# Four value buffers in linear attention's output units, and an MLP's first differences alternating with the statistics

## What is computed

```python
def rms_norm(x, g):
    y = xf * lax.rsqrt(jnp.mean(xf * xf, axis=-1, keepdims=True) + RMS_EPS)
    return (y * g.astype(jnp.float32)).astype(x.dtype)

def even_mixer(u, ...):
    ...
    o = gla_chunked(q, k, v, log_alpha)          # 4 heads of 128 value channels
    o = rms_norm(o, gla_norm_g) * jax.nn.silu(g)
    mix = jnp.concatenate([rg_out, o.reshape(bn, sn, GLA_VDIM)], axis=-1)
    return mix @ w_out

for layer in range(2):
    ...                                          # mixer or attention -> y
    x = layer_norm(ALPHA * x + gate * y, ln_g[layer, 0], ln_b[layer, 0])
    u = x * (1.0 + scale) + shift
    y = jnp.square(jax.nn.relu(u @ mlp_w1[layer] + mlp_b1[layer])) @ mlp_w2[layer] + mlp_b2[layer]
    x = layer_norm(ALPHA * x + gate * y, ln_g[layer, 1], ln_b[layer, 1])
```

## Time and profile before

| | us |
|---|---|
| median of 3 runs | 4219.9 (4216.1 to 4227.6) |
| the profiled execution, its time | 4226.8 |
| the profiled execution, its span | 4225.0 |
| TensorE busy | 3917.6 (93%) |
| VectorE busy | 2061.9 (49%) |
| GpSimd busy | 1914.0 (45%) |
| ScalarE busy | 1175.5 (28%) |
| TensorE's granted clock, mean | 0.964 of full |
| value units, first and second pass | about 347 to 384 and 485 to 522 in the span |
| openings of the MLPs | about 543 to 593 and 2315 to 2367 in the span |

### The profile page before, as it was taken

One profiled execution on the slowest core, in us unless ns is written; L12 is line 12 of the kernel. 1 busy time (PEld: TensorE's weight loads), 2 busy tenths in 40 slices (PEclk: granted clock), 3 DMA queues, 4 the chain that ended last, 5 costly groups with the idle time before them and its releaser, 6 DMA issues.

```text
span 4225.0 us, 50589 instructions
## 1 busy us (share of the span) xinstructions
PE 3917.6 (93%) x18933; PEld 3176.9 (75%) x18933; DVE 2061.9 (49%) x3073; ACT 1175.5 (28%) x1889; POOL 1914.0 (45%) x748
## 2 busy tenths in 40 slices
PE   6898889999999999999987899999999889999997
PEld 4676777788877777777775777777877667888886
DVE  6754463434444654455555521211379666444445
ACT  5322231111114444444442311111223332222222
POOL 2433267566553412222211776446555376445352
PEclk9998999999999999999998999999999899999999
DMA  6321012322310101111100111111101111111110
GB/s 209 102 70 30 26 40 85 99 84 89 99 51 22 45 26 36 31 36 36 36 21 16 41 60 49 45 40 49 51 25 55 45 50 50 40 50 50 40 59 40
DMA packets 246725, 224.65 MB, mean 53 GB/s; under 512 B 12924, under 2 KB 194850, under 8 KB 246579
## 3 DMA queue, kind: packets, MB, share of 16 engines
q1 hardware_dynamic: 222496, 171.09, 13.4%
q10 hardware_dynamic: 24083, 51.54, 3.7%
HBM read 218.34 MB, written 4.26 MB: 53 GB/s over the span
## 4 chain that ended last, share of the span: by engine, by line
PE 80%; DVE 12%; ACT 3%; issue 2%; DMA 1%; ACTq 1%; DVEq 0%
PE PS L658 11%; PE PS L660 11%; PE PS L659 11%; PE PS L784 5%; PE PS L786 5%; PE PS L785 5%; PE PS L685 3%; PE PS L687 3%; PE PS L686 3%; PE PS L1138 3%; DVE ADMS L2115 2%; PE PS L1123 1%; PE PS L1108 1%; PE PS L1070 1%; PE PS L1050 1%
## 5 line engine op out<-in xcount | busy, mean ns | idle before, releaser
L3035 POOL TENSOR_SCALAR WH<-RAW 128x1024 fp32r<-128x1024 f32 x255 | 729.9, 2862 | 1317.8 <-PE PS L687 525.3
L658 PE MATMUL PS<-UH,WH 128*128 128x512 f32 (+1 forms) x2192 | 878.7, 401 | 16.2 <-DVE UL L2156 6.3
L659 PE MATMUL PS<-UL,WH 128*128 128x512 f32 (+1 forms) x2192 | 871.4, 398 | 0.0
L660 PE MATMUL PS<-UH,WL 128*128 128x512 f32 (+1 forms) x2192 | 871.3, 398 | 0.0
L3037 POOL TENSOR_TENSOR WL<-RAW,WH 128x1024 fp32r<-128x1024 f32 x255 | 621.1, 2436 | 21.3
L658 PEld LDWEIGHTS PS<-UH,WH 128*128 128x128 f32 (+1 forms) x2192 | 414.0, 189 | 122.8 <-issue 7.7
L2126 DVE TENSOR_TENSOR X<-PS,X 128x512 f32<-128x512 f32 x432 | 292.7, 687 | 435.2 <-PE PS L786 424.0
L660 PEld LDWEIGHTS PS<-UH,WL 128*128 128x128 f32 (+1 forms) x2192 | 413.0, 188 | 103.5
L659 PEld LDWEIGHTS PS<-UL,WH 128*128 128x128 f32 (+1 forms) x2192 | 413.8, 189 | 100.1 <-issue 0.2
L784 PE MATMUL PS<-WH,HH 128*128 128x512 f32 x1024 | 405.6, 396 | 26.2 <-DVE X L2126 13.4
L786 PE MATMUL PS<-WL,HH 128*128 128x512 f32 x1024 | 400.3, 391 | 0.0
(11 more groups left out here) (358 smaller groups left out, 7178.0 us busy)
## 6 DMA issues: line engine op xcount, KB each, us to landing
RAW<-in_mlp_w_dram SPq DMA_DIRECT2D x128, 512.0 KB, 3.9
ADM<-in_ada_w_dram ACTq DMA_DIRECT2D x96, 256.0 KB, 3.3
RAW<-in_w_up_dram SPq DMA_DIRECT2D x44, 512.0 KB, 3.8
ADR<-in_ada_w_dram ACTq DMA_DIRECT2D x32, 512.0 KB, 4.3
RAW<-in_w_down_dram SPq DMA_DIRECT2D x22, 512.0 KB, 3.5
RAW<-in_ev_w_in_dram SPq DMA_DIRECT2D x20, 512.0 KB, 3.9
RAW<-in_w_in_dram SPq DMA_DIRECT2D x20, 512.0 KB, 3.9
ADS<-in_ada_w_dram SPq DMA_DIRECT2D x16, 512.0 KB, 8.8
```

What stands on the lines that cost most here:

```text
L658: pe.matmul(bank(b)[0:width], wh, xh, start=(k == 0), stop=False)
L659: pe.matmul(bank(b)[0:width], wh, xl, start=False, stop=False)
L660: mm = pe.matmul(bank(b)[0:width], wl, xh, start=False, stop=(k == NK - 1))
L3035: pool.tensor_scalar(WH[slot][:, 0:n], r[:, 0:n], 1.0, None, ALU.mult).then_inc(S("w_hi"), 1)
```

## The change

Value units: OO gets four buffers, one per unit, GSQ one instead of two, and DEC moves to a place of 64 bytes behind MASKG, since OO 3 takes its former one. ScalarE's `square` is cut in two: `copy_o` copies the bank and frees it, `square` reads OO and waits for TensorE's sum of the unit before. The order of the twelve and more ScalarE instructions changes. On VectorE gain times gate moves ahead of the reciprocal.

Openings: `ul_and_stats` takes the place of `stats` and `ul` at both places. Behind each odd block's difference it makes the two bn_stats of one block of X; the four bn_aggr come last.

```diff
--- before.py
+++ after.py
@@ -551,12 +551,12 @@
         STT_ = at("STT", [P, 16, P], e0 + 42 * KB)
         GMH = [at(f"GMH{i}", [P, SEQ], e0 + (16, 20)[i] * KB, F32R) for i in range(2)]
         GML = [at(f"GML{i}", [P, SEQ], e0 + (24, 54)[i] * KB, F32R) for i in range(2)]
-        OO = [at(f"OO{i}", [P, HALF], e0 + 50 * KB + 2 * KB * i) for i in range(2)]
-        GSQ = [at(f"GSQ{i}", [P, HALF], (top, e0 + 58 * KB)[i]) for i in range(2)]
+        OO = [at(f"OO{i}", [P, HALF], a) for i, a in enumerate((e0 + 50 * KB, e0 + 52 * KB, e0 + 58 * KB, top + 6 * KB))]
+        GSQ = at("GSQ", [P, HALF], top)
         GRS = at("GRS", [P, HALF], top + 2 * KB)
         MASKG = at("MASKG", [P, P], top + 4 * KB)
         WUP = at("WUP", [16, 256], top + 5 * KB)
-        DEC = at("DEC", [P, 16], top + 6 * KB)
+        DEC = at("DEC", [P, 16], top + 4 * KB + 512)
 
         d0 = scr[3]
         QH = at("QH", [P, SEQ], d0, F32R)
@@ -970,7 +970,7 @@
                         pe.wait_ge(S("gsq"), 4 * p + u + 1)
                         if 4 * p + u >= 2:
                             pe.wait_ge(S("gla_std"), 4 * p + u - 1)
-                        pe.matmul(bank(6 + u % 2), ONES[:, :], GSQ[u % 2][:, :], start=True, stop=True)\
+                        pe.matmul(bank(6 + u % 2), ONES[:, :], GSQ[:, :], start=True, stop=True)\
                             .then_inc(S("gla_sum"), 1)
 
                     a_free.wait_at(NA)
@@ -1631,15 +1631,14 @@
                         for h in range(2):
                             free(act.activation(B[2 + i][:, half(h)], ev_bank(("g", p, i, h)), ACT.Silu))
 
+                    def copy_o(u):
+                        free(act.activation(OO[u][:, :], ev_bank(("o", p, u)), ACT.Copy))
+
                     def square(u):
-                        b = ev_bank(("o", p, u))
-                        if u >= 2:
-                            act.wait_ge(S("m_ready"), 4 + 4 * p + u - 1)
-                        act.activation(OO[u % 2][:, :], b, ACT.Copy)
-                        act.activation(GSQ[u % 2][:, :], b, ACT.Square).then_inc(S("gsq"), 1)
-                        act.wait_ge(S("gsq"), 4 * p + u + 1)
-                        act.sem_inc(S("a_free"), 1)
-                        mine.skip()
+                        mine.wait_at(0)
+                        if u:
+                            act.wait_ge(S("gla_sum"), 4 * p + u)
+                        act.activation(GSQ[:, :], OO[u][:, :], ACT.Square).then_inc(S("gsq"), 1)
 
                     def root_o(u):
                         act.wait_ge(S("gla_sum"), 4 * p + u + 1)
@@ -1648,17 +1647,21 @@
 
                     def high_o(u):
                         go.take()
-                        act.activation(GMH[u % 2][:, half(u // 2)], OO[u % 2][:, :], ACT.Copy).then_inc(S("gmh"), 1)
-
+                        act.activation(GMH[u % 2][:, half(u // 2)], OO[u][:, :], ACT.Copy).then_inc(S("gmh"), 1)
+
+                    copy_o(0)
                     square(0)
+                    copy_o(1)
+                    root_o(0)
                     square(1)
-                    root_o(0)
+                    copy_o(2)
                     high_o(0)
+                    root_o(1)
                     square(2)
-                    root_o(1)
+                    copy_o(3)
                     high_o(1)
+                    root_o(2)
                     square(3)
-                    root_o(2)
                     high_o(2)
                     root_o(3)
                     high_o(3)
@@ -2139,6 +2142,19 @@
                     if each or tb % 4 == 3:
                         ins.then_inc(S("nv"), 1)
 
+            def ul_and_stats(n, *tbs):
+
+                for k in range(NK):
+                    ul(n, 0, k)
+                    if k % 2:
+                        tb = tbs[k // 2]
+                        for e in range(2):
+                            ins = dve.bn_stats(BST8[:, tb, 6 * e:6 * e + 6], X[:, tb, half(e)])
+                chain.done(ins)
+                for tb in tbs:
+                    ins = dve.bn_aggr(MV8[:, tb, :], BST8[:, tb, :])
+                ins.then_inc(S("nv"), 1)
+
             def xhat(h):
 
                 ns.take()
@@ -2411,14 +2427,14 @@
                     for u in range(4):
                         hh, h = u % 2, u // 2
                         dve.wait_ge(S("gsq"), 4 * p + u + 1)
+                        chain.done(dve.scalar_tensor_tensor(out=OO[u][:, :], in0=OO[u][:, :],
+                                                            scalar=pv("ev_gla_norm_g", 2 * p + hh),
+                                                            in1=B[2 + hh][:, half(h)], op0=ALU.mult, op1=ALU.mult))
                         gst.take()
                         chain.done(dve.reciprocal(GRS[:, :], GRS[:, :]))
-                        chain.done(dve.scalar_tensor_tensor(out=OO[hh][:, :], in0=OO[hh][:, :],
-                                                            scalar=pv("ev_gla_norm_g", 2 * p + hh),
-                                                            in1=B[2 + hh][:, half(h)], op0=ALU.mult, op1=ALU.mult))
-                        dve.tensor_tensor(OO[hh][:, :], OO[hh][:, :], GRS[:, :], ALU.mult).then_inc(S("gla_o"), 1)
+                        dve.tensor_tensor(OO[u][:, :], OO[u][:, :], GRS[:, :], ALU.mult).then_inc(S("gla_o"), 1)
                         gmh.take()
-                        dve.tensor_tensor(GML[hh][:, half(h)], OO[hh][:, :], GMH[hh][:, half(h)].bitcast(F32),
+                        dve.tensor_tensor(GML[hh][:, half(h)], OO[u][:, :], GMH[hh][:, half(h)].bitcast(F32),
                                           ALU.subtract).then_inc(S("m_ready"), 1)
                     if p == 0:
                         ev_add("R", p, BY_BLOCK[0] + BY_BLOCK[1])
@@ -2431,8 +2447,8 @@
                 ev_add("R", 1, BY_BLOCK[1][2:8], 10)
                 gd.skip(len(EV_ITEMS))
                 af.skip(len(EV_A))
-                stats(4, 5, 6, 7)
-                ul(1, 0, *range(NK))
+                mine.wait_at(0)
+                ul_and_stats(1, 4, 5, 6, 7)
 
             hh_ready = Tally(dve, S("hh_ready"))
 
@@ -2646,8 +2662,7 @@
                 for i in range(12, 16):
                     out_unit(7, i, (7, 4, 5, 6))
                 dve.wait_ge(S("od_b7f"), 144)
-                stats(4, 5, 6, 7)
-                ul(3, 0, *range(NK))
+                ul_and_stats(3, 4, 5, 6, 7)
 
             def spatial():
                 taps, turn_d = [0], [0]
```

## The result

The changed kernel takes 4200.3 us, the median of five runs (4197.5 to 4202.3), against 4223.9 for the kernel before in five (its first three, on which the prediction stood, had 4219.9). The ratio is 0.9943, 95% interval 0.9919 to 0.9966. The forecast was 4201.0, in a range of 4192 to 4210. Its profiled execution has a span of 4196.3 us, 28.7 less than the one before, so the two traces exaggerate the gain of 23.5 us between the medians by 5; the comparison of two traces of one and the same kernel, under Experiments, shows how far traces differ by themselves.

The account below looks back on a forecast made before the run. Mostly back-to-back TensorE matmuls (four fifths of the chain of waits) bound the kernel, so gains come only where they stop. Value units 10.1 + openings 8.8 = 18.9 us, from 4219.9 to 4201.0, range 4192 to 4210.

Parts of the forecast that it names:

- Value units, 10.1 us: Linear attention's two passes: four buffers make all periods 6.21 us, gain times gate hidden once; 5.07 us per pass.
- the first root: ScalarE's root for unit 0 of each pass: taken as 0 gain, within 0 to 0.5 us per pass.
- the 5.07 stays: Behind each value-unit pass: VectorE's additions still come last, after TensorE's banks fill, so the whole 5.07 us is kept.
- First half of an opening, 4.05 and 3.05 us: Start of each MLP: first difference UL 0 no longer waits for eight statistics, so it starts 4.05 and 3.05 us earlier.
- The late variances: MLP openings: variances come some ten us later, but the first relu waits for matmuls ending later still; costed at nothing.
- Second stretch, 8.8 us in the replay: Row vectors to second half's differences, VectorE and GpSimd lists replayed in order: openings gain 2.0 and 6.8 us overall.
- (a): First opening: TensorE's clock stays up, giving up to 3 us there; time 4196; chance 0.13.
- (b): Openings give nothing because GpSimd's splits hold the second stretch's end; gain 10.1 us, time 4209.8; chance 0.12.
- (c): Slower: each of eight two-input VectorE instructions in the second stretch meets a whole GpSimd subtraction; time 4222.7; chance 0.03.
- (d): Value units don't reach 6.21 us, paced by ScalarE or TensorE's sum; some 6 us in all, time 4207; chance 0.1.
- (e): Openings: every GpSimd instruction blocks VectorE, not the subtractions alone; gain 15.9 us, time 4204.0; chance 0.05.
- About what a measurement can tell.: Whole kernel's time: 0.3% (12.7 us) is about what a measurement can tell from no change.

Follow-up runs that it names:

- the comparison of two traces of one and the same kernel: The kernel before, profiled again with no edit: ratio 1.000 (0.9972 to 1.0029); over attention its two traces come 7.2 us apart.
- statistics last: Changed kernel with all eight bn_stats behind the eight differences instead of between them: ratio 0.9949 to the kernel before.
- root late: Changed kernel with ScalarE's square of unit 1 ahead of the root of unit 0: 4230 us.
- units and openings alone: Two runs: changed kernel with the openings undone, 4212.3 us, ratio 0.9971; kernel before with only both openings changed, ratio 0.9968.
- one-input splits: Changed kernel with GpSimd's two-input subtraction replaced by a one-input multiplication, weights' low parts left out: second stretches 15.02 and 13.21 us, against 17.29 and 14.26.
- the last comparison: Changed kernel again (0.9954, 4204.1 us), with two differences ahead of the third residual block (0.9910), and also with gain times gate before the rounded-copy wait (0.9889).

## Why the prediction was right, step by step

**Value units, 10.1 us.** The mechanism was right in each part but the first root: three equal periods, VectorE as the pace, gain times gate hidden once, additions behind remainder 3 as what TensorE waits for. The term was too small. Per pass 5.77 and 6.06 us came, 11.8 in all, for 10.1. The rest of 1.7 us is the first root, 0.56 and 0.86 us, which I had put at 0 within 0 to 0.5 on the ground that TensorE's sum doesn't move; what had been late was the table load, which needs no sum. The periods were 0.05 us shorter than taken. That "the 5.07 stays" behind a pass was not safe: from the first copy to the last addition the traces of the changed kernel give 12.3 and 10.5 us, by how many matmuls TensorE makes at half clock after its wait for the additions. TensorE's banks were full 3.25 us ahead of its resumption, not some 4.

**First half of an opening, 4.05 and 3.05 us.** Measured 3.99 and 2.98 up to UL 0, by the ends of the additions before; up to UL 7 4.3 and 2.9. The statistics fit between the pairs; one difference of eight (536.43) followed a statistic without a gap. The late variances cost nothing, as costed: statistics last, which brings them later still, lost 0.2 us.

**Second stretch, 8.8 us in the replay.** The sum came out, 1.5 and 7.4 for the 2.0 and 6.8 replayed, but the experiments say that this was partly luck. The replay itself is not written out in the prediction, so its steps can't be checked, only its lengths (17.7 and 14.8 us, measured 17.29 and 14.26). They end at the first difference; the 16.45 and 19.37 us that stand beside them end at TensorE's turning, 0.8 us later, and the like figures of the kernel before are 15.62 and 18.55, from which the gains of 2.0 and 6.8 come. The first opening's figure is stable: 45.4 to 45.7 us in the seven traces that have the change's order of additions and GpSimd's own list, against 48.1 in three of the old order. The second's depends on the phase it meets. Up to the first additions the change gave 7.2 to 7.4 us in the four traces that start at -3.1 (the changed kernel twice, root late, statistics last), and 5.6 and 1.3 in the two at -4.0. What picks between -3.1 and -4.0 is whether GpSimd's first split or VectorE's fourth scaling starts first, by 0.1 us; what else differs between the two at -4.0 is how long the MLP's first products run at half clock (2.7 and 4.4 us). The replay's rule (two-input instructions exclude each other, one-input ones block for a moment) holds in the rows; as a tool for lengths it was right to 1 us in three of the four cases replayed and off by 3 in one.

**Sum.** 11.8 (or 12.3 with what lay between the passes) + 1.5 + 7.4 make 21; the forecast had 18.9, the medians give 23.5 in one set and 18 to 19 in another (0.9954), and units and openings alone gave 12 and 13, all with intervals of 8 to 10 us either way. The predicted gain is inside each of them.

**The rivals.** (a) The clock in the first opening: blocks 2 and 3 were turned at or near the full clock (0.63 us for four, 534.20), block 4 at half (1.09). It gave 0.3 us instead of up to 3. (b) The openings give nothing: for the first opening it was nearly true, 1.1 to 1.5 of 4.05 us up to the first additions and 0.1 to 2.3 up to the MLP's middle, for the reason given, GpSimd's splits. (c) and (d) did not occur; the least slack of the value units, the root, was enough even at a period of 5.45. (e) fell by the one-input splits. By the page of the Trainium skill named there (SBUF — State Buffer, section SBUF: two separate sides) the one-input instructions would have blocked for their length; the 1.21 us beside a GpSimd instruction of 3.26 disagrees, the 2.87 us beside a two-input one agrees.

**"About what a measurement can tell."** With 0.3% I was near: the changed kernel's twelve executions in the last comparison lie between 4192 and 4224, and the intervals of a ratio were 0.3 to 0.6% wide. The traces resolve 0.05 us in the length of a pass; over longer pieces two traces of one kernel differ by 1 to 2 us even outside attention.

## What to carry to other kernels

Where two engines hand one another a shared buffer, look for the unequal periods: the pair of units that did not wait showed, before anything was changed, how long all of them could be. Work that is ready and that nobody waits for (statistics, a scaling of residuals) should stand behind the short instruction that frees a bank, and its own wait gap is the place to put it; moving two differences ahead of one residual block gave 10 us of trace for no instruction. If two engines hold up one another's instructions, as VectorE and GpSimd do here, an earlier start of one of them buys less, or more, than its own length, and only traces say which, several of them: here one and the same edit was worth 7.4, 5.6 or 1.3 us by where the two lists met. Take such a gain as a range.

## What was not expected of the hardware

The clock of TensorE in attention differs between executions of one program: 0.95 and 0.97 on average over 815 us, which is 9 us of matmul time. In two traces it ended at half clock: root late (0.50 from 2240 to 2300 us, some 30 us lost) and one-input splits (0.50 from 2160 to 2260 us, some 34 us lost). The executions of the kernel before on record lie between 4208 and 4257 us. The passes of the value units repeat to 0.02 us, but shifts of 1 to 2 us stand behind them and at the start of the first MLP's loop.

ScalarE's table load (1.28 us) doesn't wait for the data of the instruction that needs it: in the changed kernel it starts 0.02 us behind the instruction ahead of it and 0.4 us before TensorE's sum is done, in both passes. An order that lets it start beside a foreign wait hides part of it. In the kernel before's second pass it stood 0.40 us behind the instruction ahead of it all the same.

GpSimd's one-input instructions (2.77 us alone) delayed VectorE's two-input ones only as long as some 1.9 us of them or more were left, by up to 0.84 us; its two-input instructions delayed them for nearly all that was left of them (up to 2.25 us). VectorE's one-input scaling of 0.81 us took 1.52 beside the start of a one-input instruction of GpSimd.
